# Six small loads moved behind ACT's copies of the state, a first weight unit in two halves, and one tile's scaling moved to ACT

## What is computed

```
h    = rmsnorm(x) * ln_mix
proj = h @ w_in                 # columns: u_a 1024, u_b 1024, z 1024, x/B/C 1536, dt 16
v    = silu(layernorm(causal_dwconv(conf_state, u_a * sigmoid(u_b), width 31)))
xBC  = silu(causal_dwconv(ssm_state, xbc, width 4))
y    = gated, grouped rmsnorm of ssd_scan(xBC, softplus(dt + dt_bias), -exp(a_log), h0) + d * x
x    = x + concat(v, y) @ w_out
x    = x + top-2 experts of 8 in the top-1 of 4 groups, SwiGLU, on rmsnorm(x) * ln_ffn
y    = rmsnorm(x) * ln_final
```

## Time and profile before

| | us |
|---|---|
| median of 3 runs | 791.07 (790.22 to 792.41) |
| the profiled execution: its time | 792.5 |
| the profiled execution: its span | 790.8 |
| TensorE busy in it | 756.9 (96%) |
| VectorE, ACT, GpSimd busy | 272.6, 154.9, 140.5 |
| moved by DMA | 249.58 MB, 316 GB/s in the mean |

### The profile page before, as it was taken

How to read it: one execution, slowest core, us unless ns; L and a number is a source line. 1 busy time by engine, 2 the same in 40 slices (tenths; PEclk the granted TensorE clock), 3 DMA queues, 4 the chain that set the end, 5 groups by cost and what they waited for, 6 DMA issues and landing times.

```text
span 790.8 us, 8695 instructions
## 1 busy us (share of the span) xinstructions
PE 756.9 (96%) x3470; PEld 366.1 (46%) x3470; DVE 272.6 (34%) x629; ACT 154.9 (20%) x308; POOL 140.5 (18%) x168
## 2 busy tenths in 40 slices
PE   6899999999999999999999999999999999999986
PEld 4666677768843335533333333333333333333332
DVE  2299399994756523620111011011101101101103
ACT  3201121236622002201111111111012101101103
POOL 3169999522002000000000000000000000000000
PEclk9899999999999999699999999999999999999998
DMA  9981430041749686999999999999999999999993
GB/s 310 308 303 68 156 114 1 0 116 41 254 174 296 209 299 265 334 360 416 429 426 426 427 426 425 427 427 426 428 428 424 428 427 425 424 430 426 427 385 108
DMA packets 51400, 249.58 MB, mean 316 GB/s; under 512 B 6982, under 2 KB 24422, under 8 KB 38671
## 3 DMA queue, kind: packets, MB, share of 16 engines
q1 hardware_dynamic: 45460, 243.40, 77.0%
q10 hardware_dynamic: 3371, 2.81, 1.3%
q0 software_dynamic: 2528, 2.79, 1.1%
HBM read 246.87 MB, written 8.61 MB: 323 GB/s over the span
## 4 chain that ended last, share of the span: by engine, by line
PE 91%; DMA 3%; issue 2%; DVE 2%; SPq 2%; ACT 0%; POOLq 0%; DVEq 0%
PE bank L1211 27%; PE bank L808 18%; PE bank L1234 14%; PE bank L1074 9%; PE bank L1259 9%; DMA xcx<-in_state_conf_conv 2%; PE bank L1194 2%; SPq L488 1%; PE bank L1212 1%; PE bank L1063 1%; PE bank L1223 1%; PE bank L1032 1%; PE bank L903 1%; PE bank L1120 1%; PE bank L1045 0%
## 5 line engine op out<-in xcount | busy, mean ns | idle before, releaser
L808 PE MATMUL bank<-region_a,ring 128*128 128x320 f32 x576 | 158.1, 435 | 0.8 <-DVE region_a L1654 0.8
L1654 DVE TENSOR_TENSOR region_a<-region_a,bank 64x512 f32<-64x512 f32 (+1 forms) x33 | 22.4, 680 | 366.0 <-ACT region_a L1581 366.0
L1211 PE MATMUL bank<-ring,zz 128*64 128x512 f32 x288 | 126.9, 593 | 8.5 <-issue 8.4
L808 PEld LDWEIGHTS bank<-region_a,ring 128*128 128x128 f32 x576 | 109.3, 191 | 46.5 <-issue 1.6
L1212 PE MATMUL bank<-ring,zz 128*64 128x512 f32 x288 | 128.3, 599 | 0.0
L1655 DVE SCALAR_TENSOR_TENSOR bank<-region_a,par,bank 128x256 f32<-128x256 f32 x232 | 91.2, 477 | 0.0
L761 POOL DMA_INDIRECT region_a<-hn_scratch,region_a x16 | 16.0, 999 | 382.0 <-PE bank L1194 367.7
L1259 PE MATMUL bank<-zz,masks 128*128 128x512 f32 (+1 forms) x192 | 81.3, 610 | 0.0
L1211 PEld LDWEIGHTS bank<-ring,zz 128*64 128x64 f32 x288 | 38.5, 137 | 89.9 <-issue 89.9
L1074 PE MATMUL bank<-ring,x_v_y 128*128 128x512 f32 (+1 forms) x192 | 74.0, 605 | 0.0
L1581 ACT ACTIVATE region_a<-bank 64x512 f32<-64x512 f32 x32 | 18.9, 590 | 248.6 <-PE bank L1212 248.6
(11 more groups left out here) (313 smaller groups left out, 783.5 us busy)
## 6 DMA issues: line engine op xcount, KB each, us to landing
ring<-in_expert_w_up SPq DMA_DIRECT2D x18, 2048.0 KB, 31.5
ring<-in_expert_w_down SPq DMA_DIRECT2D x18, 2048.0 KB, 27.8
ring<-in_expert_w_gate SPq DMA_DIRECT2D x17, 2048.0 KB, 38.2
ring<-in_w_in SPq DMA_DIRECT2D x9, 2048.0 KB, 15.3
x_v_y<-in_expert_w_down SPq DMA_DIRECT2D x5, 2048.0 KB, 38.6
x_v_y<-in_expert_w_gate SPq DMA_DIRECT2D x5, 2048.0 KB, 30.2
x_v_y<-in_expert_w_up SPq DMA_DIRECT2D x5, 2048.0 KB, 26.6
ring<-in_w_out SPq DMA_DIRECT2D x4, 2048.0 KB, 10.0
```

Of the source, the lines that this page charges most:

```text
L808: ins = pe.matmul(pt[0:m, 0:T], w[:, k, :], ht[:, k, :], start=k == 0, stop=k == KD - 1)
L1211: pe.matmul(to[0:CAP, :], x[:, k, :], wg[:, FE * k:FE * k + FE], **st)
L1654: tt_ = lambda out, a, b, op: dve.tensor_tensor(out, a, b, op)
```

## The change

Four edits:

- SyncE loads the first unit in two halves of the contraction (k 0 to 3 and 4 to 7); the first has a semaphore of its own. TensorE waits for it ahead of tile b0, and for the second half ahead of that tile's fifth step.
- The third tile of x is scaled by ACT (activation Copy with a scale) in place of VectorE's tensor_scalar. VectorE takes the reciprocal between the two halves of tile 0's gain.
- ACT no longer waits for ub0. Its five small loads and the load of wdt are issued after its copies of the convolution state, ahead of glu_parts(2).
- x_gain takes a list of halves.

```diff
--- before.py
+++ after.py
@@ load_unit (SyncE)
+                if n == 0:
+                    sp_.dma_start(dst[:, 0:KD // 2, :], src[:, 0:KD // 2, :]).then_inc(S("first_unit"), 16)
+                    dst, src = dst[:, KD // 2:, :], src[:, KD // 2:, :]
                 sp_.dma_start(dst, src).then_inc(ring_in[n % R], 16)
@@ project (TensorE)
+                first = name == ("in", "b", 0)
                 if unit is None:
                     w, m = wdt, H
+                elif first:
+                    pe.wait_ge(S("first_unit"), 16)
+                    w, m = ring[:, 0, :].rearrange("p (k c) -> p k c", k=KD)[:, :, 0:P], P
...
                 for k in range(KD):
+                    if first and k == KD // 2:
+                        landed(pe, unit)
@@ ACT
-            act.wait_ge(ring_in[0], 16)
-            ld = lambda dst, src: act.dma_start(dst, src).then_inc(S("ssm_in"), 16)
-            row = lambda name, n: A[name][0:1, :].to_broadcast([P, n])
-            ld(dtb[:, :], row("ssm_dt_bias", H))
-            ld(alog[:, :], row("ssm_a_log", H))
-            for hh in range(2):
-                ld(dsk[64 * hh:64 * hh + 64, :], A["ssm_d"][0:1, hh:H:2].to_broadcast([HD, NC]))
-            ld(lnffn[:, :], A["ln_ffn"].rearrange("a (p k) -> (a p) k", k=KD))
+            act.wait_ge(S("rinv_in"), 1)
+            act.activation(xt[0:TS, 2, :], xt[0:TS, 2, :], ACT.Copy, scale=rst[0:TS, 5:6]).then_inc(S("xn"), 1)
...
             act.wait_ge(filled, J[("xt", 2, 1)] + 1)
-            act.dma_start(wdt, w_in[:, :, C_DT:C_DT + H]).then_inc(S("wdt_in"), 16)
             glu_parts(0)
... (the copies of par and of the states)
+            (the five loads, word for word)
+            act.dma_start(wdt, w_in[:, :, C_DT:C_DT + H]).then_inc(S("wdt_in"), 16)
             glu_parts(2)
@@ VectorE
-            x_gain(0)
-            x_scaled(2)
+            x_gain(0, [0])
+            dve.wait_ge(S("rt"), 3)
+            dve.reciprocal(rst[:, 5:6], rst[:, 2:3]).then_inc(S("rinv_in"), 1)
+            x_gain(0, [1])
             x_gain(1)
             x_gain(2)
```

## The result

The changed kernel takes **800.88 us** in the median of four executions (798.67 to 806.89) against 790.64 for the kernel before: a ratio of 1.0128, interval 1.0099 to 1.0157. It is slower by 10.2 us, where +2.2 was forecast, and it lies outside the range of 785.0 to 796.5. The profiled execution is the slowest of the four.

The account below looks back on a forecast made before the run. TensorE's first 60 us were taken to set the time, front shifts passing one for one to the transfer-bound experts' stage. Terms -5.7 + 4.9 + 3.0 = +2.2 us gave 793.3 us; range 785 to 796.5.

Parts of the forecast that it names:

- the columns' wait: TensorE ahead of the dt tile: time-step columns land at 54.6 but are wanted at 49.7, a wait of 4.9 us.
- Parts 1 and 2: Front: third x tile on ACT and first unit halved let the first projection start at 12.1, gaining 0.4 us.
- rival 2: Parameter rows slow by themselves: wait at 30 us and its clock stay, only 0.4 gained; +4.3, 795.4 us; chance 10%.
- Part 3a: Front: small loads off ACT's early queue let parameter rows land about 27, ending TensorE's 2.44 us wait.
- term of 2.44 us: TensorE's wait from 29.97 to 32.41 for the last parameter load, counted as wholly gained.
- the clock's 2.85: Parameter transposes and tile b2 at full clock once the parameter wait is gone: 2.05 + 0.8 = 2.85 us gained.
- the clock goes with the wait: Claim that the low clock until 39 us vanishes with TensorE's parameter wait, worth 2.85 us.
- 5.7 us of gains: Forecast gains in the front: 0.4 earlier start, 2.44 parameter wait, 2.85 clock.
- Part 3b: Small loads behind ACT's state copies: issued 35.2 to 39.0, columns land at 54.6, so TensorE waits 4.9 us.
- The low clock behind the wait: TensorE's work behind its wait for the columns runs at low clock: 3.0 us lost, bounds 0 and 4.
- Rival 1: Columns land in time for the dt tile, so only the gains stand: 785.4 us, faster; chance 25%.

Follow-up runs that it names:

- wdt_early: Changed kernel with only the time-step columns' load (wdt) issued in its old place, the other five small loads still late; 792.55 us, ratio 1.0.
- after_b: The changed kernel, unaltered, executed and profiled a second time; parameter wait 2.53 us, columns' wait 7.09 us, dt matmuls start at 59.29 us.
- the move alone: Kernel before with only ACT's six small loads moved behind its copies of the state; 800.82 us, ratio 1.0122.
- before_b: The kernel before, unaltered, executed and profiled a second time; parameter wait 0.37 us, dt matmuls start at 52.62 us.
- before_c: The kernel before, unaltered, executed and profiled a third time; parameter wait 0.16 us, dt matmuls start at 51.99 us.

## Why the prediction was wrong

**What bounds, and what passes.** Right: the front's shift reached the router one for one (9.47 in the profile; the starts of the dt matmuls and of the router's stage are 254.0 to 254.4 us apart in every execution without the columns' wait). The forecast's direction was right, and the columns' wait with its low clock was the named cause.

**Parts 1 and 2.** The start was forecast at 12.1; it was 12.76, 12.08 and 12.08. But the 0.4 us were counted as a gain, in rival 2 too, and they aren't one: the parameters set when TensorE goes on, at 32.0 to 32.7 in all but one (wdt_early, 33.2) of the executions of kernels that load the 31 rows in one piece.

**Part 3a is the step that failed first.** "If its stretch shrinks by 0.15/0.26 it ends at 25.7 ... So the wait goes." q1 without q10 beside it moved 54 packets instead of 58, and the wait was 2.43, 2.53 and 0.74 us in three profiles, ending at 32.7, 32.1 and 32.4. The slow stretch was the parameter rows' own: of q1's 58 packets there 48 have 4 KB, and such a packet takes 0.28 us in the median before and 0.29 after. So the term of 2.44 us, and the clock's 2.85 behind it, hung on a cause that was not there. The trace of before could have told. In the answer from which the earlier trace rows come, q10 has this row (before, 19 to 20 us):

```profile
q10 hardware_dynamic: 52, 0.00, 6.0%
```

Its packets took 6.0% of the engines' time and q1's own 96.0%; by these shares, taking q10 away could give back about 6%, and 0.15/0.26 asked for 40%. This was rival 2, at 10%. It gave +4.3 us, still short of what came.

**The clock at 33 us, and the baseline.** "Together 2.05 + 0.8 = 2.85 us" was right for the profiled execution and wrong for the median. Two further executions of before wait only 0.37 and 0.16 us and do not have this low clock, and after_b has the wait without it: "the clock goes with the wait" was read from one execution. Of 5.7 us of gains the mean of three profiles on each side shows 0.2 us lost: TensorE was ready for the columns at 52.2 to 55.85, 53.5 in the mean, against 53.35 for the same point before. This is the largest error, some 5.9 us.

**Part 3b.** Right: ACT's first issue, forecast 35.2, was at 35.12 and 35.39 where no low clock came first, and the last one ended at 38.80, as forecast 39.0. Mis-sized: the time from the first issue to the landing, 19.4 forecast (3.6 + 15.8), 23.8 to 25.3 measured, inside the bounds (27.05), with the wrong mechanism. It was worked out as turns of 0.104 us a pair with both queues full. The engines in fact stood idle most of the time (share 0.25, 0.30), and both queues suffered. The landing depends on the 4-byte packets ahead of the columns: 19.5 to 21.2 us from the columns' issue with them ahead, 11.1 to 12.2 without, in the same late place. In the earlier trace rows the same packets (143 of the 153 are of 4 bytes) had run beside 2 KB ones at full share, so the rows gave no warning of an idle engine; why the engines are full in the one place and idle in the other, no run shows. But the rows did have the number: before, the columns took 24.0 us from their issue and 27.05 from the first. The move hardly shortened that time. It took away the 16 us by which they were early. The wait was 6.7 to 7.3 us against 4.9.

**The low clock behind the wait.** Forecast 3.0 us. The dt matmuls took 6.20, 5.79 and 6.88 us against 4.48: 1.8 in the mean, and no more than that shows at the router.

**The sum as it should have stood**, from the means of three profiles on each side: 7.05 (wait) + 1.8 (clock) + 0.15 (ready later) = 9.0 us; the router's stage starts at 316.33 against 307.45, 8.9 later. The medians say 10.2 for the change and 9.1 for the move alone. The 1.3 us between 8.9 and 10.2 lie within the interval of the ratio (7.8 to 12.4 us), and no run explains them.

**Rival 1** (the columns land in time) did not come. 11.1 us is the shortest landing of the columns, 21.2 the longest behind ACT's late issues. The Trainium skill, "DMA: Bandwidth & Descriptors" (Anatomy of one DMA), fits about 2.0 us plus bytes at 436 GB/s to a DMA that GpSimd issues; an estimate by that is 2.2 us for 64 KB. ACT issues the columns, beside a busy queue, and no run here came near it.

**Open.** Why the gather of hn_scratch has two durations: in the long ones its first packet comes 2.3 to 3.1 us behind the issue instead of 1.7 to 2.1, and its packets are spread over 3 us and more instead of 0.9 to 1.4. Nothing that was changed here decides it, and nothing was tried on it. What makes the first matmuls slow in a third of the executions is open too: the granted clock shows it in before_b and before_c, and not in the others.

## What to carry to other kernels

Before a wait in the first microseconds is counted as a gain, profile the kernel before a second and a third time: a low clock that stood at 33 us in one execution and at 14 us in two others went with a wait of 2.4 us in the one and of 0.4 and 0.2 in the others, and 5.3 of the 5.7 us of forecast gains stood on it. A load whose last dimension is strided is dear not by its bytes but by its packets, and the one who pays is the transfer behind it in the queue and everything beside it; order such loads last, or load whole rows and pick out of them on chip. To blame one transfer for the slowness of another, look first at the share of the engines' time that each takes in the same stretch: 6.0% could not explain 40%. And a load that is moved later may take as long as before; count the time it took in its old place first.

## What the runs showed of the hardware

- Two loads of 512 packets of 4 bytes, with the 1024 of 64 bytes of the columns behind them, left the 16 DMA engines at a share of 0.25 to 0.30 for 3 to 6 us; together with the other queue, which had 2 MB units waiting, they moved 61 to 78 GB/s. With the 1024 small ones replaced by 128 of 64 bytes the share was 1.06 and the rate 388 GB/s.
- Issuing the same two loads held ACT for 1.3 to 1.7 us, and once for 4.26; the next issue behind them took 0.64 to 0.67 us, and once 3.29, where it takes 0.46 to 0.48 with no 4-byte load ahead.
- A load of 31 rows (124 KB) set TensorE's time at 32 us; in two loads of 16 and 15 rows the last packet of 4 KB or more ended 5.7 us earlier (25.8 against 31.5) and TensorE did not wait.
- Three executions of one program, the kernel before, differ by 3.4 us in their front (52.0 to 55.4 us for the same matmul). A gather takes 3.5 to 3.8 or 6.1 to 7.8 us, and two programs showed one in one execution and the other in the next; the time behind the router's start is 3.3 us longer in the mean with the long one. Whether this makes the kernel before spread from 788 to 795 us isn't shown: its three profiles all have the short one.
- Waits of TensorE of 2.5 to 2.6 us left the granted clock at 1.00 in three executions; waits of 2.4 to 3.7 us had a low clock behind them in four others.
